# Block compression of the sample stage: four 64x64 matmuls instead of one block-diagonal 128x128 matmul

## The reference, cut to what matters

```python
def comp(x, w, pe):
    blocks = x[:, idx] + pe[:, None, :]                      # idx: (63, 32)
    return jnp.einsum('bnlgd,lde->bnge', blocks, w.reshape(CMP_BLK, HEAD_DIM, HEAD_DIM))

kc = rms_norm(comp(k_raw, cmp_w[0], cmp_pe[0]), kn_cmp)
vc = comp(v_raw, cmp_w[1], cmp_pe[1])
```

## Time and profile before

| | |
|---|---|
| median of 3 runs | 2543.5 us (2542.39 to 2547.15) |
| span of the profiled execution, first to last instruction | 2535.2 us |
| TensorE matmuls busy | 2072.4 us (82%) |
| TensorE weight loads busy | 1344.6 us (53%) |
| VectorE busy | 976.3 us (39%) |
| ScalarE busy | 566.6 us (22%) |
| GpSimd busy | 118.7 us (5%) |
| stage `sample_c`, 988 to 1326 us of the span | 338 us |

### The profile page before, as it was taken

The page is one execution under the profiler, slowest core; times in us unless marked ns, Lnnn a source line. Parts: engine busy times, 40 slices in busy tenths (PEclk is TensorE's granted clock), DMA queues, the critical chain, the costliest instruction groups (busy, mean ns, idle before and its releaser), DMA issues. The chain is left out here.

```text
span 2535.2 us, 32455 instructions
## 1 busy us (share of the span) xinstructions
PE 2072.4 (82%) x9999; PEld 1344.6 (53%) x10000; DVE 976.3 (39%) x2516; ACT 566.6 (22%) x1292; POOL 118.7 (5%) x174
## 2 busy tenths in 40 slices
PE   7899999688566762999977999999499739999991
PEld 4454555355354552878866777877445314444440
DVE  1221222122188884044434555555233413333334
ACT  1111111211122220022214565555211101111110
POOL 0000000000000001000000000000000030000004
PEclk9999999899766655699997799999799869999996
DMA  7111111444300003322315433322333516775226
GB/s 258 50 45 39 43 50 45 150 141 160 126 11 21 21 22 51 101 67 88 88 49 168 162 113 107 103 99 91 115 101 101 190 34 232 280 260 197 89 83 228
DMA packets 180897, 277.29 MB, mean 109 GB/s; under 512 B 42284, under 2 KB 147532, under 8 KB 180284
## 3 DMA queue, kind: packets, MB, share of 16 engines
q1 hardware_dynamic: 167500, 203.59, 25.3%
q0 software_dynamic: 8704, 55.85, 6.1%
q10 hardware_dynamic: 4608, 16.78, 1.6%
HBM read 226.59 MB, written 78.95 MB: 121 GB/s over the span
## 5 line engine op out<-in xcount | busy, mean ns | idle before, releaser
L218 PE MATMUL p_acc<-p_w,p_hT 128*128 128x384 f32 (+2 forms) x1152 | 419.9, 527 | 27.2 <-DVE p_hT L276 27.2
L218 PEld LDWEIGHTS p_acc<-p_w,p_hT 128*128 128x128 f32 x1152 | 223.1, 194 | 222.5 <-issue 146.0
L2226 PE MATMUL m_hid<-m_w,m_xT 128*128 x512 | 237.0, 617 | 13.2 <-DMA m_w<-in_moe_w 10.4
L1023 PE MATMUL pa_sc<-pa_kT,pa_qT 128*128 128x512 f32 (+4 forms) x528 | 197.4, 480 | 1.1 <-ACT pa_qT L1078 1.1
L1048 PE MATMUL pa_op<-pa_v,pa_pT 128*128 128x64 f32 (+1 forms) x1452 | 196.2, 278 | 0.0
L1162 DVE CUSTOM_DVE_ANT_0 pa_p<-pa_sc,pa_mask 128x256 f32<-128x256 f32 (+7 forms) x192 | 117.3, 611 | 195.4 <-PE pa_sc L1023 116.9
L1048 PEld LDWEIGHTS pa_op<-pa_v,pa_pT 128*128 128x128 f32 (+1 forms) x1452 | 184.4, 198 | 11.2 <-issue 10.0
L2226 PEld LDWEIGHTS m_hid<-m_w,m_xT 128*128 128x128 f32 x512 | 97.8, 196 | 133.7 <-issue 133.7
L2170 PE MATMUL m_acc<-m_wo,m_catT 128*128 128x512 f32 (+1 forms) x288 | 134.8, 624 | 9.6 <-DVE m_st L2462 5.8
L1105 ACT ACTIVATE pa_p<-pa_p,pa_nb 128x256 f32<-128x256 f32 (+7 forms) x192 | 126.2, 657 | 73.1 <-DVE pa_nb L1165 72.6
L2607 DVE COPY m_xT<-m_tp 128x512 f32<-128x512 f32 x32 | 22.1, 692 | 297.3 <-PE m_tp L2218 297.3
(11 more groups left out here) (353 smaller groups left out, 2505.4 us busy)
## 6 DMA issues: line engine op xcount, KB each, us to landing
m_w<-in_moe_w SPq DMA_DIRECT2D x48, 1024.0 KB, 9.8
sa_kv<-in_cache_a SPq DMA_DIRECT2D x20, 1536.0 KB
out_a_s<-in_cache_a POOLq DMA_DIRECT2D x8, 3048.0 KB
sc_x<-in_cache_c SPq DMA_DIRECT2D x136, 128.0 KB
tmp_ys<-m_cat ACTq DMA_DIRECT2D x16, 512.0 KB, 2.9
tmp_ys<-m_x ACTq DMA_DIRECT2D x16, 512.0 KB, 3.2
p_w<-in_w_in SPq DMA_DIRECT2D x4, 1536.0 KB, 11.3
p_w<-in_w_in SPq DMA_DIRECT2D x3, 2048.0 KB, 17.1
```

Source lines behind the costliest of these rows:

```text
L218: last = pe.matmul(acc[c % 4][:, 0:cw], hT[:, k, :], w[:, k, c0:c0 + cw], start=k == 0, stop=k == KD - 1)
L1023: last = pe.matmul(sc[u % 2][:, lo:hi], qT[s][:, j, pr, :], kT[x][:, kp, k0 * C + lo:k0 * C + hi], start=True, stop=True)
L2226: last = pe.matmul(hid[s][:, :], xT[:, k, :], w13[:, bass.ds(e % WB * KD + k, 1), :].rearrange("p o n -> p (o n)"), start=k == 0, stop=k = ...
```

## The change

The map is kept once for each kv head (`wc[r, k, n, :]`, 64x64, the same for partitions 0 to 63 and 64 to 127), without zeros; the memset of `wc` and the wait for it are gone. Each step n of `compress` now makes four matmuls of 64 rows: kv head g takes row tile g and writes to a bank of its own (`cps` or `ms`), and keys and values (k) take a column tile each, partitions 0 to 62 and 64 to 126 of both banks. Keys and values are made together, so the pieces are cut anew: 8, 6, 6 and 12 steps; no piece is left for after the transposes of the large probabilities. The three small results go to `tp[0]`. The bias is made for one head only (64 weight columns and 64 rows), and VectorE adds it to both heads by broadcast, reading both banks in one instruction.

```diff
@@ -1456,11 +1456,11 @@
         ps = lambda name, shape: ctx.enter_context(nc.psum_tensor("sc_" + name, shape, F32))
         sem = ctx.enter_context(semaphores(nc, "sc_"))
         ident = sb("ident", [P, P])
-        wc = sb("wc", [P, 2, 32, P])
+        wc = sb("wc", [P, 2, 32, HD])
         peT = sb("peT", [P, 2, 32])
-        peb = sb("peb", [P, 2])
-        pebw = sb("pebw", [P, 2, NCMP])
-        pebr = sb("pebr", [NCMP, 2, P])
+        peb = sb("peb", [HD, 2])
+        pebw = sb("pebw", [HD, 2, NCMP])
+        pebr = sb("pebr", [NCMP, 2, HD])
         gain = sb("gain", [P, 1])
         share = sb("share", [NCMP, NB + 1])
         rsum = sb("rsum", [NR, NR])
@@ -1491,7 +1491,9 @@
         st = sb("st", [NR, 3, 4])
         o = [sb(f"o{s}", [NR, 3, HD]) for s in range(2)]
         tp = [ps(f"tp{n}", [P, 512]) for n in range(2)]
-        cps, ms = ps("cps", [P, 512]), ps("ms", [P, 512])
+        cm = ps("cm", [P, 1024])
+        cps, ms = cm[:, 0:512], cm[:, 512:1024]
+        both = lambda rs: cm[rs, :].rearrange("p (g n) -> p g n", g=2)[:, :, 0:HD]
         sS, sW, sM = ps("sS", [P, 1024]), ps("sW", [P, 512]), ps("sM", [P, 512])
         const_in, seen, settled, zero, qtp, q_ev, pes, peb_in, pr_out = map(sem, (
             "const_in", "seen", "settled", "zero", "qtp", "q_ev", "pes", "peb_in", "pr_out"))
@@ -1530,10 +1532,9 @@
                 for a, b in ((ident, "ident"), (share, "share"), (rsum, "rsum"), (idx, "blk"),
                              (mnew, "mask_new"), (mwin, "mask_sw")):
                     sp.dma_start(a[:, :], t[b][:, :]).then_inc(const_in, 16)
-                sp.wait_ge(zero, 3)
                 for g in range(2):
                     r = slice(HD * g, HD * g + HD)
-                    sp.dma_start(wc[r, :, :, r], t["c_cmp_w"][0].rearrange("k (l r) e -> r k l e", r=HD)
+                    sp.dma_start(wc[r, :, :, :], t["c_cmp_w"][0].rearrange("k (l r) e -> r k l e", r=HD)
                                  ).then_inc(const_in, 16)
                     sp.dma_start(peT[r, :, :], t["c_cmp_pe"][0].rearrange("k l d -> d k l"),
                                  allow_slow_non_contiguous=True).then_inc(const_in, 16)
@@ -1608,7 +1609,6 @@
             def _(pool):
                 pool.memset(qz[:, :, :], 0.0).then_inc(zero, 1)
                 pool.memset(kcr[:, :], 0.0).then_inc(zero, 1)
-                pool.memset(wc[:, :, :, :], 0.0).then_inc(zero, 1)
 
             @block.tensor
             def _(pe):
@@ -1621,12 +1621,12 @@
                 last.then_inc(qtp, 1)
                 for k in range(2):
                     for n in range(32):
-                        last = pe.matmul(cps[:, k:k + 1], wc[:, k, n, :], peT[:, k, n:n + 1],
+                        last = pe.matmul(cps[0:HD, k:k + 1], wc[0:HD, k, n, :], peT[0:HD, k, n:n + 1],
                                          start=n == 0, stop=n == 31)
                 last.then_inc(pes, 1)
                 pe.wait_ge(peb_in, 3)
                 for k in range(2):
-                    last = pe.transpose(cps[0:NCMP, k * P:(k + 1) * P], pebw[:, k, :], ident[:, :])
+                    last = pe.transpose(cps[0:NCMP, k * HD:(k + 1) * HD], pebw[:, k, :], ident[0:HD, 0:HD])
                 last.then_inc(pes, 1)
                 pe.wait_ge(q_ev, 6)
                 pe.wait_ge(peb_in, 4)
@@ -1646,20 +1646,22 @@
                             last = pe.transpose(tp[n % 2][:, c * P:(c + 1) * P], row(c, n % 2, n // 2), ident[:, :])
                         pe_c.did(last, f"tc{n}")
 
-                def compress(m, k, lo, hi):
-
-                    if k == 0 and lo == 0:
+                def compress(m, lo, hi):
+
+                    if lo == 0:
                         act_c.after(pe, m, "tc3")
                         if not (isinstance(m, int) and m == 0):
                             dve_s.after(pe, m - 2, "out")
-                    if k == 1 and lo == 0:
-                        dve_s.after(pe, m - 1, "i2")
+                            dve_c.after(pe, m - 1, "kcT")
                         pe.sem_inc(settled, 1)
-                    out = ms[0:NCMP, 320:320 + P] if k else cps[0:NCMP, 0:P]
                     for n in range(lo, hi):
-                        last = pe.matmul(out, xT[:, 2 * k + n % 2, n // 2:n // 2 + 8 * (NCMP - 1) + 1:8],
-                                         wc[:, k, n, :], start=n == 0, stop=n == 31)
-                    if k == 1 and hi == 32:
+                        for k in range(2):
+                            for g, bank in ((0, cps), (1, ms)):
+                                r = slice(HD * g, HD * g + HD)
+                                last = pe.matmul(bank[HD * k:HD * k + NCMP, 0:HD],
+                                                 xT[r, 2 * k + n % 2, n // 2:n // 2 + 8 * (NCMP - 1) + 1:8],
+                                                 wc[r, k, n, :], start=n == 0, stop=n == 31)
+                    if hi == 32:
                         pe_c.did(last, "comp")
 
                 def transpose_keys(m):
...
@@ -1712,20 +1712,19 @@
                     else:
                         xc_in[1 - s].wait(pe, fill + s, 16 * 8)
                     transpose_pairs(n + 1, 1 - s, 0, 4)
-                    compress(n + 1, 0, 0, 8)
+                    compress(n + 1, 0, 8)
                     dve_s.after(pe, n, "pc")
                     pe.sem_inc(settled, 1)
-                    pe_s.did(pe.transpose(ms[0:NCMP, 192:192 + NR], pc[:, :], ident[0:NR, 0:NR]), "tpc")
-                    compress(n + 1, 0, 8, 16)
+                    pe_s.did(pe.transpose(tp[0][0:NCMP, 0:NR], pc[:, :], ident[0:NR, 0:NR]), "tpc")
+                    compress(n + 1, 8, 14)
                     dve_s.after(pe, n, "pcT")
                     pe.sem_inc(settled, 1)
-                    pe_s.did(pe.matmul(ms[0:NR, 256:256 + NB + 1], pcT[:, :], share[:, :], start=True, stop=True), "imp1")
-                    compress(n + 1, 0, 16, 24)
+                    pe_s.did(pe.matmul(tp[0][0:NR, 64:64 + NB + 1], pcT[:, :], share[:, :], start=True, stop=True), "imp1")
+                    compress(n + 1, 14, 20)
                     dve_s.after(pe, n, "i1")
                     pe.sem_inc(settled, 1)
-                    pe_s.did(pe.matmul(ms[0:NR, 288:288 + NB + 1], rsum[:, :], imp[:, :], start=True, stop=True), "imp2")
-                    compress(n + 1, 0, 24, 32)
-                    compress(n + 1, 1, 0, 24)
+                    pe_s.did(pe.matmul(tp[0][0:NR, 96:96 + NB + 1], rsum[:, :], imp[:, :], start=True, stop=True), "imp2")
+                    compress(n + 1, 20, 32)
                     dve_s.after(pe, n, "pS")
                     pe.sem_inc(settled, 1)
                     for c in range(8):
@@ -1737,7 +1736,6 @@
                         pe.transpose(tp[1][:, c * NR:(c + 1) * NR], pW[:, c * P:(c + 1) * P], ident[0:NR, 0:NR])
                     pe.transpose(tp[1][0:DEC_S, 256:256 + NR], pW[:, CWIN:NKW], ident[0:NR, 0:NR])
                     pe_s.did(pe.transpose(tp[1][0:DEC_S, 320:320 + NR], pS[:, PAST:NKS], ident[0:NR, 0:NR]), "tpw")
-                    compress(n + 1, 1, 24, 32)
                     act_s.after(pe, n, "tps")
                     dve_s.after(pe, n, "tpw")
                     if not last:
...
@@ -1815,12 +1813,12 @@
                     c.open(dve)
                 dve.wait_ge(const_in, 16 * 13)
                 dve.wait_ge(pes, 1)
-                dve.tensor_copy(peb[:, :], cps[:, 0:2]).then_inc(peb_in, 1)
+                dve.tensor_copy(peb[:, :], cps[0:HD, 0:2]).then_inc(peb_in, 1)
                 dve.wait_ge(peb_in, 1)
                 for k in range(2):
-                    dve.tensor_copy(pebw[:, k, :], peb[:, k:k + 1].to_broadcast([P, NCMP])).then_inc(peb_in, 1)
+                    dve.tensor_copy(pebw[:, k, :], peb[:, k:k + 1].to_broadcast([HD, NCMP])).then_inc(peb_in, 1)
                 dve.wait_ge(pes, 2)
-                dve.tensor_copy(pebr[:, :, :], cps[0:NCMP, 0:2 * P].rearrange("p (k e) -> p k e", k=2)
+                dve.tensor_copy(pebr[:, :, :], cps[0:NCMP, 0:2 * HD].rearrange("p (k e) -> p k e", k=2)
                                 ).then_inc(peb_in, 1)
                 dve.wait_ge(peb_in, 4)
 
@@ -1834,8 +1832,10 @@
 
                     step = stepper(dve_c, m)
                     pe_c.after(dve, m, "comp")
-                    step("kcf", dve.tensor_tensor(kcf[:, :], cps[0:NCMP, 0:P], pebr[:, 0, :], ALU.add))
-                    step("vc", dve.tensor_tensor(vc[s][:, :], ms[0:NCMP, 320:320 + P], pebr[:, 1, :], ALU.add))
+                    bias = lambda k: pebr[:, k, :].unsqueeze(1).to_broadcast([NCMP, 2, HD])
+                    by_head = lambda a: a[:, :].rearrange("p (g e) -> p g e", g=2)
+                    step("kcf", dve.tensor_tensor(by_head(kcf), both(slice(0, NCMP)), bias(0), ALU.add))
+                    step("vc", dve.tensor_tensor(by_head(vc[s]), both(slice(HD, HD + NCMP)), bias(1), ALU.add))
```

(14 more changed lines are left out.)

## The result

In the measurement that the prediction was made for, the changed kernel took 2526.6 us (median of four executions, 2523.4 to 2529.5) against 2545.3: a ratio of 0.9912, 95% interval 0.9887 to 0.9937. (The ratios are those on record for the runs; the medians alone give 0.9926 and 0.9891.) Forecast were 2516.5, 27 us less than before; by the medians the two measurements gave 19 and 28. The profiled execution has a span of 2521.3 us, 13.9 less than before. The stage itself gave 27 us: from its first instruction to the first matmul of prompt attention are 323.5 us instead of 350.2. Prompt attention, which the change doesn't touch, then took 18 us longer; its length varies from one execution to the next.

The account below looks back on a forecast made before the run. TensorE and the VectorE chain bound the loop body by turns, with SyncE's queue right beside. Terms -3.7 - 13.7 - 7.7 - 21.6 + 19.6 = -27.1 took 2543.5 to 2516.5 us, own range 2505 to 2532.

Parts of the forecast that it names:

- Start: Start of the stage: no memset wait before the weight load, -3.7 us; bias matmuls of 64 columns, -13.7 us.
- Pace: Compression matmuls: four tiles run abreast, each bound by its own stepped weight load, 0.24 us per step.
- The two bounds: Limits on the compression pace: 0.12 us per step from moving columns, 0.96 with eight loads one after another.
- taking turns: Compression rival: the four tiles are served one after another, 0.96 us per step, 2667 us; 0.11 together with a low clock.
- groups of four within some 20 ns: Expected sign in the compression: its weight loads come in groups of four within some 20 ns.
- Sample 0: Compression of sample 0, alone on TensorE before the loop: 15.6 becomes 7.9 us, -7.7 us.
- A body without the clock: Loop body: -1.3 us before the block scores, -1.4 for the removed tail piece; -2.7, eight times -21.6 us.
- The clock: Loop: TensorE idles 4.3 us after compression, its clock falls; 2.8 us per spell in seven bodies, +19.6 us.
- The queue: SyncE's page loads: the loop can gain about 37 us, 38 with the last body, until it waits for loads.
- rival that SyncE's round sets the body now: Loop, rival stated for e11: SyncE's round sets the body; moving stores gives bodies of 28 to 29 us; no chance given.
- The sum: Whole kernel: start, sample 0, bodies and clock together change the time by -27.1 us, to 2516.5 us.
- two of the rivals: Loop bound by SyncE's queue, 2505.5 us, chance 0.17; compression's column tiles unable to overlap stepped loads, 2543 us, chance 0.17.

Follow-up runs that it names:

- e2: Kernel before with only the start changed: off-diagonal weight blocks zeroed, no wait for it, bias matmuls of 64 columns; 2535.7 us, ratio 0.9953.
- e1: Changed kernel plus extra compression series of one, two or four tiles; stepped reads 0.24 us per step, contiguous with one or two tiles 0.115 to 0.12.
- e3: Changed kernel with 28 unused transposes behind each body's last compression piece, to fill TensorE's idle gap; 2511.9 us, ratio 0.9882.
- e10: Changed kernel with four unused 128x512 matmuls and one of 256 columns behind each body's last compression piece; 2507.1 us, ratio 0.9821.
- e12: Changed kernel with e10's filling matmuls and GpSimd instead of SyncE issuing the six stores per sample; 2506.1 us, ratio 0.9836.
- e7: Changed kernel with every compression tile matmul issued twice; median 2565.5 us.
- e9: Changed kernel's order and start, but with the old block-diagonal 128x128 compression weights; 2562.9 us, ratio 1.0054.
- e11: Changed kernel with the six stores of each sample issued by GpSimd instead of SyncE; 2521.4 us, ratio 0.9886.
- second measurement: Changed kernel, unchanged, timed again against the kernel before in more rounds; 2523.0 against 2550.8 us, ratio 0.9882.
- e13: e12 with ScalarE writing xT in reading order, so compression weight loads are contiguous, and two more filling matmuls; 2499.3 us, ratio 0.9808.

## Why the prediction was right, point by point

- *Start.* -3.7 and -13.7 forecast, 17.4 together. Measured 17.8 at the first transposes, 0.9 of it ahead of the stage, so 16.9; 18.2 and 1.4 in e2, so 16.8. Bias matmuls 13.81 us, forecast 13.7.
- *Pace.* 0.24 us per step was called the weakest step, and it held to the digit, by its own mechanism (e1). The two bounds are real as well: 0.115 to 0.12 is the pace with contiguous loads, and taking turns (0.96) doesn't happen in any pairing. The sign "groups of four within some 20 ns" came only in part: three loads start within 14 ns, the fourth some 45 ns behind. The kernel gets a factor of two, since the load and not the moving operand sets its pace. The Trainium skill's rule of a factor per small dimension (TensorEngine Tiling (Array Packing), section "Theoretical Speedup") agrees in that four tiles cost what one does, 7.89 against 7.71 us. The Trainium skill's penalty for accesses that each touch a new line (SBUF — State Buffer, section "Door 1: The DMA port swizzle") agrees with 7.7 against 3.8 us.
- *Sample 0.* -7.7 forecast, 15.6 to 8.34 measured.
- *A body without the clock.* -2.7 forecast. The second to sixth bodies of e3, e10 and e12 at full clock are 27.6 to 27.8 us against 30.6 to 30.8: -3.0. The parts were off in opposite ways: line 1726 comes 1.4 earlier (forecast 1.3), and the first half shrinks by 2.0, because the compression behind line 1726 outlasted the softmax before (it ended at 1242.12 + 5.92 = 1248.04, the softmax at 1247.3); the term took the softmax for the longer. The second half shrinks by 0.9 to 1.2, forecast 1.4.
- *The clock.* +2.8 per spell forecast, 2.9 measured, behind an idle stretch of 4.36 us (forecast 4.3). The size came out, in part by luck: it was priced on a spell ahead of and in the first body of the kernel before (33.5 us at 0.92, so 5.4 us at 0.50), while a body of the changed kernel is at 0.50 for about 10 us (30.6 at 0.83), much of it over idle TensorE. The reason was too narrow: e7 and e9 show spells behind 0.5 to 1.5 us of idle time, and e10 two behind no more than 0.9. The forecast's own sum puts the end of compression at 1241.6, not 1241.7. The forecast's "7 x 2.8" nearly cancels the seven bodies' gain, and so it is: 33.5 + 184.1 = 217.6 us from the first scores to the last before, 214.4 after.
- *The queue.* The gain would end at 37 to 38 us: e10, where loads are waited for, ended at 36.4, and e12, with the stores taken off the queue, at 43.9. The rival that SyncE's round sets the body now is refuted by e11.
- *The sum.* -27.1 forecast. From the stage's first instruction to prompt attention's first matmul it is -26.7 in the first pair of profiles, -27 over all five; the timed gain was 19 in the first measurement and 28 in the second. The prediction names two ranges, 2505 to 2532 for its own theory and 2502 to 2545 with two of the rivals in; 2526.6 and 2523.0 lie in both. What no term held is the clock of prompt attention, 449 to 467 us in five profiles, as large as the whole change. It took 18 us of the gain in the first pair of profiles.

## What to carry to other kernels

Before packing small matmuls into tiles, find what sets their pace: here it was a step of 8 in the stationary operand (shown for the tiles by e1; for the kernel before by its equal 0.120 us per record only). Tiles let four loads run abreast but don't shorten one; a contiguous copy halves the step once more, and was worth 1.5 us of a first half of 19.3 (e13), though no clear gain in time. Whether it would have paid without the tiles was not run. Here, time saved on TensorE, which then waited, was paid back in part by its clock, so look at the second half of a loop body, not only at the part that was made shorter. And where a stage behind the change varies by more than the effect, measure at the end of the changed stage, in at least two profiles of each kernel.

## What the runs showed of the hardware that I had not expected

- A stepped weight load keeps its pace at either clock: 0.24 us per step at 0.50 and at 1.00 (e1), while four contiguous tiles with 16 moving columns need 0.21 per step (6.96 us for 252 of 256 records) at 0.50, against 0.12 at 1.00 with 64. So the stepped compression loses nothing in a spell of low clock; a contiguous read halves the time of a step at full clock and gains about a tenth at half of it, by these series.
- 64-row matmuls of other tiles slip into each other: lines 1722 and 1726 (0.18 us) start within 0.01 us of the next compression records. Before, the three small ones took 1.05 us beside 24 matmuls, 0.35 each; now it is 1.54 us from 1208.60 to 1210.14 for 48 records (1.44) and one small matmul, 0.1.
- TensorE lost up to 2.0 us at a time to waits that the profile names "issue": with contiguous loads in e13 and e1, and with stepped ones in e7, 1.9 us ahead of the scores. What they wait for was not found.
